# Sample attention of a decoder step: four heads in four groups of output partitions, scores over four pages at once

## What is computed

```
def _diff_attn_sample(q, k, v, k_past, v_past, lam):
    l_new, p_len = q.shape[1], k_past.shape[1]
    scale = HEAD_DIM ** -0.5
    s_past = jnp.einsum('bqhd,bkhd->bhqk', q, k_past, preferred_element_type=jnp.float32) * scale
    s_new = jnp.einsum('bqhd,bkhd->bhqk', q, k, preferred_element_type=jnp.float32) * scale
    causal = jnp.tril(jnp.ones((l_new, l_new), dtype=bool))
    s_new = jnp.where(causal, s_new, -jnp.inf)
    a = _diff_weights(jnp.concatenate([s_past, s_new], axis=-1), lam).astype(v.dtype)
    out = (jnp.einsum('bhqk,bkhe->bqhe', a[..., :p_len], v_past, preferred_element_type=jnp.float32)
           + jnp.einsum('bhqk,bkhe->bqhe', a[..., p_len:], v, preferred_element_type=jnp.float32))
    return out.astype(v.dtype)
```

## Time and profile before

| | |
|---|---|
| median of 3 runs | 1553.23 us (1553.16 to 1554.63) |
| profiled execution: span from first to last instruction | 1539.1 us |
| median of the runs less that span | 14.1 us |
| profiled execution: mean granted TensorE clock | 0.937 |
| sample attention in it, from the first key transposes to the last values | 648.5 to 854.8 us |
| TensorE busy, products | 1306.9 us, 85% of the span |
| VectorE, ScalarE, GpSimd busy | 744.7, 568.3, 283.7 us |

### The profile page before, as it was taken

How to read it: one execution, slowest core, us unless ns; L and a number is a source line. 1 busy time by engine, 2 the same in 40 slices (tenths; PEclk the granted TensorE clock), 3 DMA queues, 4 the chain that set the end, 5 groups by cost and what they waited for, 6 DMA issues and landing times.

```text
span 1539.1 us, 20098 instructions
## 1 busy us (share of the span) xinstructions
PE 1306.9 (85%) x5769; PEld 883.9 (57%) x5770; DVE 744.7 (48%) x1101; ACT 568.3 (37%) x786; POOL 283.7 (18%) x289
## 2 busy tenths in 40 slices
PE   4879999999997799789999899638989989899920
PEld 1334444366665466566565688426767777677720
DVE  4863232201113887511011454567865556888747
ACT  4530111000001556422232122206755546777633
POOL 0020000010000111000000011112554344554424
PEclk9989999999998999999999899758999999999965
DMA  8981200011100200077664311406875765888545
GB/s 288 367 318 32 82 28 26 16 46 42 41 0 0 84 1 1 1 233 237 193 173 126 127 41 42 183 16 247 303 269 200 272 251 218 313 303 324 216 157 184
DMA packets 84544, 230.86 MB, mean 150 GB/s; under 512 B 16101, under 2 KB 28517, under 8 KB 72165
## 3 DMA queue, kind: packets, MB, share of 16 engines
q1 hardware_dynamic: 70288, 203.80, 37.6%
q0 software_dynamic: 14192, 26.24, 4.8%
HBM read 220.42 MB, written 34.21 MB: 165 GB/s over the span
## 4 chain that ended last, share of the span: by engine, by line
PE 64%; DVE 10%; DMA 9%; issue 7%; ACT 5%; POOL 2%; DVEq 2%; ACTq 1%; SPq 1%; POOLq 0%
PE psum L530 19%; PE psum L583 12%; PE psum L611 11%; PE psum L690 4%; DMA xg<-h_scratch,gidx 4%; PE psum L517 4%; PE psum L705 2%; PE psum L629 2%; DMA wada<-in_w_ada_dram 2%; PE psum L638 2%; DVE xgL L1493 1%; ACT pexp L922 1%; DVEq L332 1%; PE psum L672 1%; DMA wgu<-in_w_up_dram 1%
## 5 line engine op out<-in xcount | busy, mean ns | idle before, releaser
L583 PE MATMUL psum<-wqkv,hT 128*128 128x512 f32 (+1 forms) x432 | 187.5, 594 | 0.0
L611 PE MATMUL psum<-hT,wcv 128*128 128x352 f32 x576 | 170.9, 459 | 0.0
L1485 DVE TENSOR_TENSOR wguL<-wgu,wguH 128x2048 fp32r<-128x2048 f32 x64 | 146.7, 2294 | 39.9 <-ACT wguH L1034 39.2
L530 PE MATMUL psum<-wguH,xgH 128*128 128x512 f32 x320 | 130.8, 409 | 33.0 <-DVE xgL L1493 33.0
L611 PEld LDWEIGHTS psum<-hT,wcv 128*128 128x128 f32 x576 | 109.3, 190 | 60.6
L583 PEld LDWEIGHTS psum<-wqkv,hT 128*128 128x128 f32 (+1 forms) x432 | 77.8, 182 | 103.2 <-issue 103.1
L1034 ACT CAST wguH<-wgu 128x2048 fp32r<-128x2048 f32 x64 | 120.3, 1912 | 23.5 <-issue 14.2
L530 PE MATMUL psum<-wguH,xgL 128*128 128x512 f32 x320 | 126.7, 396 | 0.0
L530 PE MATMUL psum<-wguL,xgH 128*128 128x512 f32 x320 | 126.4, 395 | 0.0
L1553 POOL TENSOR_SCALAR small<-small 128x1 f32<-128x1 f32 (+3 forms) x36 | 20.1, 559 | 508.4 <-ACT ajunk L1011 213.5
L629 PE MATMUL psum<-kT,qz 128*128 128x512 f32 (+3 forms) x192 | 77.7, 520 | 19.5 <-ACT pexp L922 18.2
(11 more groups left out here) (269 smaller groups left out, 2412.1 us busy)
## 6 DMA issues: line engine op xcount, KB each, us to landing
wgu<-in_w_gate_dram SPq DMA_DIRECT2D x32, 1024.0 KB, 4.9
wgu<-in_w_up_dram SPq DMA_DIRECT2D x32, 1024.0 KB, 7.5
wdn<-in_w_down_dram SPq DMA_DIRECT2D x32, 1024.0 KB, 7.4
wada<-in_w_ada_dram SPq DMA_DIRECT2D x24, 1024.0 KB, 8.2
kseq<-in_cache_k_dram SPq DMA_DIRECT2D x64, 256.0 KB, 3.0
vseq<-in_cache_v_dram SPq DMA_DIRECT2D x64, 256.0 KB
yg<-y_scratch SPq DMA_DIRECT2D x16, 512.0 KB, 4.9
wqkv<-in_w_in_dram SPq DMA_DIRECT2D x1, 6144.0 KB, 25.3
```

The costliest lines, as they stand in the source:

```text
L530: ins = mm(out, r32(x(c)), r32(w(c)), start=(begin and c == 0 and k == 0), stop=(end and c == chunks - 1 and k == 2))
L583: last = mm(psum[0:n, 2 + j, :], hT[:, c, P * t:P * t + n], wqkv[:, c, AW * j:AW * j + AW], start=(c == 0), stop=(c == DC - 1))
L611: last = mm(psum[:, 3 * (n % 2) + j, 0:TB], wcv[i % 2][:, c, j, :], hT[:, c, TB * tb:TB * tb + TB], start=(c == 0), stop=(c == DC - 1))
L1485: TT(r32(wguL[slot][:, g, :, :]), wgu[slot][:, g, :, :], wguH[slot][:, g, :, :], ALU.subtract).then_inc(S["wguL_done"], 1)
```

## The change

Each head's 32 query columns now write their own 32 output partitions of PSUM, `psum[32 * c:32 * c + 32, ...]`, so nothing accumulates over heads in the scores, and each head's values are multiplied by its own 32 weight columns alone (128 columns of values instead of 512). The keys of four pages are gathered in one buffer `kTg` of 8 KB a partition (two of them, the second on the place of the `shift_f` and `scale_f` rows), and one product takes scores for all four pages (512 columns). Maxima, exponentials, sums and `pairs` now run on 128 partitions, of which 8 in every 32 are used; the constants are laid out for that.

TensorE's list is written in another order. The second half of a sequence's scores and its new scores stand after the first page of the next sequence, the weight columns after its sixth, the values after its eighth. VectorE takes maxima, pairs and weights of the same sequence one after the other. SyncE waits for all scores before it loads the `shift_f` rows.

```diff
...
     put("valid", ok.astype(np.float32))
-    r = np.arange(SUBS * LNEW)
-    put("dmask", np.where(np.arange(LNEW)[None, :] <= (r % LNEW)[:, None], 0.0, NEG).astype(np.float32))
+    head, r = np.divmod(i, 32)
+    used = r < 2 * LNEW
+    put("dmask", np.where(used[:, None] & (np.arange(LNEW)[None, :] > (r % LNEW)[:, None]), NEG, 0.0).astype(np.float32))
     cols = np.arange(HEADS * LNEW)
-    put("pair", ((r // (2 * LNEW))[:, None] * LNEW + (r % LNEW)[:, None] == cols[None, :]).astype(np.float32))
-    put("sub0", ((r // LNEW) % 2 == 0).astype(np.float32)[:, None])
-    put("sub1", ((r // LNEW) % 2 == 1).astype(np.float32)[:, None])
+    put("pair", (used[:, None] & (head[:, None] * LNEW + (r % LNEW)[:, None] == cols[None, :])).astype(np.float32))
+    put("sub0", (used & (r // LNEW == 0)).astype(np.float32)[:, None])
+    put("sub1", (used & (r // LNEW == 1)).astype(np.float32)[:, None])
     put("tilecol", i[:, None].astype(np.float32))
...
         qbd = at("qbd", O_W + 24 * K, [P, NSEQ, 4, 32])
-        kTp = [at(f"kTp{i}", O_H + 24 * K + 2 * K * i, [P, 4, P]) for i in range(2)]
-        pdec = [at(f"pdec{i}", O_H + 4 * K * i + 512 * i, [32, PAGES * P + LNEW]) for i in range(2)]
+        kTg = [at(f"kTg{i}", o, [P, 4, 4 * P]) for i, o in enumerate((O_H + 20 * K, O_AB))]
+        pdec = [at(f"pdec{i}", O_H + 4 * K * i + 512 * i, [P, PAGES * P + LNEW]) for i in range(2)]
         aTs = [at(f"aTs{i}", O_H + 9 * K + 5 * K * i, [P, PAGES + 1, P]) for i in range(2)]
-        snew = [at(f"snew{i}", O_H + 19 * K + 64 * i, [32, LNEW]) for i in range(2)]
-        pairs = [at(f"pairs{i}", O_H + 19 * K + 128 + 64 * i, [32, 16]) for i in range(2)]
+        snew = [at(f"snew{i}", O_H + 19 * K + 64 * i, [P, LNEW]) for i in range(2)]
+        pairs = [at(f"pairs{i}", O_H + 19 * K + 128 + 64 * i, [P, 16]) for i in range(2)]
         orow = at("orow", O_X + 32 * K, [NSAMP, HEADS, P])
...
+            sp.wait_ge(W["dscore_ps"], 2 * NSEQ)
             load_mod(sp, "shift_f", shift_p, shift_s, S["sub2_rows_in"])
...
-        def page_scores(pe, s, p):
-
-            n = s * PAGES + p
-            pe.wait_ge(W["kp_sb"], n + 1)
-            if p == 0 and s >= 2:
+        def half_scores(pe, g):
+
+            s, half = divmod(g, 2)
+            pe.wait_ge(W["kp_sb"], 4 * g + 4)
+            if half == 0 and s >= 2:
                 pe.wait_ge(W["dexp_done"], 2 * s - 2)
             for c in range(4):
-                last = nc.tensor.matmul(psum[0:32, 2 * (s % 2) + p // 4, P * (p % 4):P * (p % 4) + P], qbd[:, s, c, :], kTp[n % 2][:, c, :],
-                                        start=(c == 0), stop=(c == 3))
+                last = nc.tensor.matmul(psum[32 * c:32 * c + 32, 2 * (s % 2) + half, :], qbd[:, s, c, :], kTg[g % 2][:, c, :],
+                                        start=True, stop=True)
             last.then_inc(S["dscore_ps"], 1)
...
-            def sample_values(s):
+            def new_scores(s):
+                if s >= 1:
+                    pe.wait_ge(W["dnew_done"], s)
+                for c in range(4):
+                    last = mm(psum[32 * c:32 * c + 32, 7, 256:256 + LNEW], qbd[:, s, c, :], kTs[:, c, LNEW * s:LNEW * s + LNEW], start=True, stop=True)
+                last.then_inc(S["ds_ps"], 1)
+
+            def weight_columns(s):
                 pe.wait_ge(W["pair_done"], s + 1)
-                pe.wait_ge(W["dnew_done"], min(s + 2, NSEQ))
+                if s >= 1:
+                    pe.wait_ge(W["da_sb"], s)
                 for p in range(PAGES + 1):
                     m = P if p < PAGES else LNEW
                     last = mm(psum[0:m, 7, 16 * p:16 * p + 16], pdec[s % 2][:, P * p:P * p + m], pairs[s % 2][:, :], start=True, stop=True)
                 last.then_inc(S["da_ps"], 1)
+
+            def sample_values(s):
+
                 pe.wait_ge(W["da_sb"], s + 1)
                 pe.wait_ge(W[f"vseq_in{s % 2}"], 16 * (PAGES + 1) * (s // 2 + 1))
-                for p in range(PAGES + 1):
-                    if p < PAGES:
-                        last = mm(psum[:, 6, :], aTs[s % 2][:, p, :], vseq[s % 2][:, p, :], start=(s == 0 and p == 0), stop=False)
-                    else:
-                        last = mm(psum[:, 6, :], aTs[s % 2][0:LNEW, p, :], vnew[s % 2][:, :], start=False, stop=(s == NSEQ - 1))
+                for p in range(PAGES):
+                    for h in range(HEADS):
+                        r = slice(32 * h, 32 * h + 32)
+                        mm(psum[r, 6, 0:P], aTs[s % 2][:, p, r], vseq[s % 2][:, p, P * h:P * h + P], start=(s == 0 and p == 0), stop=False)
+                for h in range(HEADS):
+                    r = slice(32 * h, 32 * h + 32)
+                    last = mm(psum[r, 6, 0:P], aTs[s % 2][0:LNEW, PAGES, r], vnew[s % 2][:, P * h:P * h + P], start=False, stop=(s == NSEQ - 1))
                 last.then_inc(S["do_ps"], 1)
...
                     last.then_inc(S["kp_ps"], 1)
-                    if p >= 1:
-                        page_scores(pe, s, p - 1)
-                page_scores(pe, s, PAGES - 1)
-                if s >= 2:
-                    pe.wait_ge(W["da_sb"], s - 1)
-                for c in range(4):
-                    last = mm(psum[0:32, 7, 256:256 + LNEW], qbd[:, s, c, :], kTs[:, c, LNEW * s:LNEW * s + LNEW], start=(c == 0), stop=(c == 3))
-                last.then_inc(S["ds_ps"], 1)
-                if s >= 1:
-                    sample_values(s - 1)
+                    if p == 0 and s >= 1:
+                        half_scores(pe, 2 * s - 1)
+                        new_scores(s - 1)
+                    if p == 4:
+                        half_scores(pe, 2 * s)
+                    if p == 5 and s >= 1:
+                        weight_columns(s - 1)
+                    if p == 7 and s >= 1:
+                        sample_values(s - 1)
+            half_scores(pe, 2 * NSEQ - 1)
+            new_scores(NSEQ - 1)
+            weight_columns(NSEQ - 1)
             sample_values(NSEQ - 1)
...
                     act.wait_ge(W["kp_ps"], n + 1)
-                    if n >= 2:
-                        act.wait_ge(W["dscore_ps"], n - 1)
-                    nc.scalar.copy(kTp[n % 2][:, :, :], psum[:, 4 + n % 2, :].rearrange("p (c n) -> p c n", c=4)).then_inc(S["kp_sb"], 1)
+                    if n >= 8:
+                        act.wait_ge(W["dscore_ps"], n // 4 - 1)
+                    nc.scalar.copy(kTg[(n // 4) % 2][:, :, P * (p % 4):P * (p % 4) + P], psum[:, 4 + n % 2, :].rearrange("p (c n) -> p c n", c=4)).then_inc(S["kp_sb"], 1)
                 act.wait_ge(W["dmax_done"], s + 1)
                 if s >= 2:
                     act.wait_ge(W["da_ps"], s - 1)
                 b, m = s % 2, dmx[:, 3 + s % 2:4 + s % 2]
-                A(pdec[b][:, 0:PAGES * P], psum[0:32, 2 * b:2 * b + 2, :].rearrange("p b n -> p (b n)"), ACT.Exp, bias=m,
+                A(pdec[b][:, 0:PAGES * P], psum[:, 2 * b:2 * b + 2, :].rearrange("p b n -> p (b n)"), ACT.Exp, bias=m,
                   accum_out=dl[:, 0:1]).then_inc(S["dexp_done"], 1)
...
             for h in range(HEADS):
-                nc.scalar.copy(orow[:, h, :], psum[32 * h:32 * h + 32, 6, P * h:P * h + P]).then_inc(S["oT_sb"], 1)
+                nc.scalar.copy(orow[:, h, :], psum[32 * h:32 * h + 32, 6, 0:P]).then_inc(S["oT_sb"], 1)
             act.wait_ge(W["oT_sb"], 4)
...
                             r = slice(64 * u, 64 * u + 64)
-                            a = 8 * c + 4 * u
+                            a = LNEW * u
                             last = nc.vector.tensor_copy(qbd[r, :, c, a:a + LNEW], qTs[r, c, :].rearrange("p (s q) -> p s q", s=NSEQ))
...
                 dve.wait_ge(W["ds_ps"], s + 1)
-                TT(snew[b][:, :], psum[0:32, 7, 256:256 + LNEW], C("dmask", 32), ALU.add).then_inc(S["dnew_done"], 1)
+                TT(snew[b][:, :], psum[:, 7, 256:256 + LNEW], C("dmask"), ALU.add).then_inc(S["dnew_done"], 1)
                 dve.wait_ge(W["dnew_done"], s + 1)
-                RED(dmx[:, 0:1], psum[0:32, 2 * b:2 * b + 2, :].rearrange("p b n -> p (b n)"), AX_X, ALU.max)
+                RED(dmx[:, 0:1], psum[:, 2 * b:2 * b + 2, :].rearrange("p b n -> p (b n)"), AX_X, ALU.max)
                 link(RED(dmx[:, 1:2], snew[b][:, :], AX_X, ALU.max))
...
                 link(TT(dr[:, 1:2], dr[:, 0:1], sgn, ALU.mult))
-                TS(pairs[s % 2][:, :], C("pair", 32), dr[:, 1:2], None, ALU.mult).then_inc(S["pair_done"], 1)
+                TS(pairs[s % 2][:, :], C("pair"), dr[:, 1:2], None, ALU.mult).then_inc(S["pair_done"], 1)
             dve.wait_ge(W["attT_ps"], 8)
             for b in range(2):
                 link(nc.vector.memset(aTs[b][:, :, :], 0.0))
             for s in range(NSEQ):
                 sample_maxima(s)
-                if s >= 1:
-                    sample_weights(s - 1)
                 sample_pairs(s)
-            sample_weights(NSEQ - 1)
+                sample_weights(s)
```

(6 more changed lines are left out.)

## The result

The changed kernel takes 1506.78 us (median of 4 runs, 1499.01 to 1510.02) against 1553.2 of before in the same comparison (1547.95 to 1554.63): ratio 0.9721, 95% interval 0.9674 to 0.9769. The profiled execution took 1510.02 us with a span of 1508.2.

The account below looks back on a forecast made before the run. TensorE was taken to bound the stage, at 22.5 us per sequence after the change against 25.3; the projection starts 15.8 earlier, so span 1539.1 - 15.8 = 1523.3, plus 14.1 gives 1537.4 us, range 1514 to 1561.

Parts of the forecast that it names:

- H: TensorE's four score products of half a sequence: 3.5 us without overlap, 0.9 with all heads overlapping, 2.2 as forecast.
- V: TensorE's value products of one sequence: 7.9 us without overlap, 3.7 with all heads overlapping, 4.9 as forecast.
- between: Scores and values: only one head's second instruction overlaps the next head's first; sequence 20.5 us before clock; forecast's chance 0.49.
- The floor of 0.05: TensorE's scores and values: a weight load with its product takes at least 0.05 us, holding a sequence's values at 3.7.
- all four overlap: Rival for scores and values: all heads run beside each other, SyncE bounds at 18.3 us; minus 37, 1516 us; chance 0.17.
- The account of the cycle: TensorE's time from one second half of scores to the next: 2H + V + 11.2 us, 20.5 as forecast.
- one fall of the clock: TensorE at half clock after a stall, 1.7 us; one per sequence and a second in every third, 2.0 added.
- the one long wait of the fourth sequence's pages: SyncE's queue: these keys issued from 700.7, landing at 707.3 where TensorE wanted them at 701; happens once.
- After that 18.3 is below 22.5: Later sequences: SyncE's issue of keys and values, 18.3 us, stays shorter than the forecast sequence of 22.5.
- Tail: End of the stage: values end at 837 against 854.8, output-weight rests at 839.7, projection starts at 840.5, not 856.26.
- No overlap: Rival for scores and values: no heads run beside each other; projection at 867.7, plus 11.5, 1565 us; chance 0.26.
- The reference: Whole kernel: median of before lies 14.1 us above its profiled span, added unchanged to the forecast span of 1523.3.

Follow-up runs that it names:

- s_one_group: Changed kernel with the scores of all heads accumulating in output partitions 0 to 31 (sample attention not computed): 1527.55 us, 0.9861 of before.
- v_heads_outer: Changed kernel with the values' loop order swapped, heads outside and pages inside: 1514.90 us, 0.9792 of before.
- paced: Changed kernel with router weights before the stage, values on GpSimd's queue and held back, three output-weight rests earlier, output weights loaded in four parts: 1478.60 us, 0.9567 of before.
- both_serial: Changed kernel with heads outermost in the values and all heads' scores in partitions 0 to 31 (sample attention not computed): 1546.01 us, 1.0001 of before.
- b_again: The kernel before, unchanged, run once more for a second profile with its own time: 1551.19 us.
- early_and_pool: Changed kernel with router weights issued before the stage and the values' pages issued by GpSimd's queue: 1490.95 us, 0.9620 of before.

## Why the prediction was right about the sign and wrong about the size

- **The step that failed** is the choice among the three cases for H and V. I took the "between" case, because "instructions on the same partitions never overlap in the earlier trace rows" and nothing in the earlier trace rows "forces a queue". In the trace four products of four heads start 7 ns apart (728.703, .710, .716, .723) and the other four 0.45 later; on one group, in `s_one_group`, such instructions start 0.43 apart. So all four heads run beside each other, and the pairs of a product don't space them. H measured 748.75 - 747.86 = 0.9 until the next product (forecast 2.2) and V 2.3 (4.9). `v_heads_outer` and `s_one_group` show that order and partitions decide it. So TensorE's own cycle came to some 17 us instead of 22.5, below SyncE's 18.75, and the projection started 172.0 us after the first key transposes instead of 840.5 - 648.5 = 192.0.
- The floor of 0.05 for a load and its product, taken from the new scores in the earlier trace rows, was no floor: 72 value instructions in 2.3 are 0.03 each. It fell together with the first step, since those new scores wrote one group of partitions.
- **The rival "all four overlap"** (0.17) was what happened, nearly to its numbers: SyncE bounds, 18.4 us per sequence worked out and 18.75 measured, projection 819 - 648.5 = 170.5 us after the first keys and 172.0 measured. Its time, 1516, was still 9 too slow, for the reason in the last point here. My chance for it was too small.
- **The page of the Trainium skill that spoke for it**, TensorEngine Tiling (Array Packing), Key Properties (tiles load and multiply independently), agrees: starts 7 ns apart. The rule of the Trainium skill, TensorE: Matmul & The Clock Gate, part 3 (a weight load overlaps products in flight only for another row group) doesn't hold here: the heads share all 128 rows, and 64 weight loads of 110 ns and their product instructions fit in 1.96 us.
- **The account of the cycle was right** apart from H and V. With the measured ones, 2 x 0.9 + 2.3 + 11.2 = 15.3, and 1.7 for one fall of the clock makes 17.0; `paced`, whose last sequences wait for no transfer, has 17.2.
- **SyncE**: the one long wait of the fourth sequence's pages came as forecast (keys issued at 703.13, forecast 700.7; values of the third sequence end at 727.4, forecast 730), and it was longer because TensorE was there sooner. "After that 18.3 is below 22.5" fell with the first step.
- **Tail**: the pause near 4 us (4.48), the clock below 1.00 in every sequence, the mod rows at no cost, the rests of the output weights as the next thing late (9.15, TensorE waits 5.6): all seen. The projection's own path lost 1.3, where I wrote nothing: from its first product to the second tile's 839.27 - 821.90 = 17.4 against 872.34 - 856.26 = 16.1, its first 5.7 us being at half clock, where before it was some 3.4.
- **No overlap**: I had it 11.5 slower; `both_serial`, which is that case, is equal to before. Its sequences take 24.6 to 26.8 us where I worked out 27.1: V is 6.3 there and not 7.9, for the reason told with the experiments.
- **The reference** failed as a second step: the 14.1 us were added as a constant, but the profiled execution of before was itself short, as `b_again` shows. Of the 30.6 us between the forecast and the median, 15.1 lie in the span (1523.3 against 1508.2), 12.3 in this constant (1.8 in the changed kernel's profile), and 3.2 come from the profiled execution lying above the median. From its stage of 212.6 the change takes off 40.6, and the two profiles' times differ by 41.2.

## What to carry to other kernels

Small fp32 products that share their rows can be spread over groups of 32 output partitions, and neighbours in the program should be of different groups: here that made 64 instructions three times as fast, and the wrong loop order gave two thirds of the gain back (a sequence's values took 8.2 us before, 2.3 in the changed kernel, 6.3 with the heads outermost). Once TensorE's part of a cycle is cut, look at once at the issuing queue: seventeen issues of 1.1 us each are a cycle of their own. And a load that is not due yet should not be issued as soon as it can be, when the engines are full, because it takes them from one that is.

## What the runs showed of the hardware that I had not expected

- Products on four groups of output partitions start 7 ns apart. Within one group 128-column value instructions start 0.109 us apart; on alternating groups 64 of them take 1.96 us, 0.03 each.
- An instruction for an idle group can start before an earlier one for a busy group: new scores at 760.27 us, the last score instruction at 760.70 (`s_one_group`).
- The second queue brought no bandwidth once the engines were full: with both queues issuing, share 1.00 at 373 GB/s, a page of keys landed after 4.5 us in the median of the stage (`early_and_pool`) instead of 2.9 (the changed kernel).

```profile
kseq<-in_cache_k_dram SPq DMA_DIRECT2D x51, 256.0 KB, 4.5
```
```profile
kseq<-in_cache_k_dram SPq DMA_DIRECT2D x51, 256.0 KB, 2.9
```
